# RWKV-7 chunks: level 5, the join, bonus and centring as 64x64 products on other quarters of the array

## What is computed

```python
def step(S, inp):                              # per token and head, S is 64 x 64
    sa = einsum('hvk,hk->hv', S, -kk_t)
    S = S * w_t[:, None, :] + sa[..., None] * b_t[:, None, :] + v_t[..., None] * k_t[:, None, :]
    o = einsum('hvk,hk->hv', S, r_t)
mu = mean(o, -1); var = mean(square(o - mu), -1)              # over the 64 of a head
o = (o - mu) * rsqrt(var + LNX_EPS) * lnx_w + lnx_b
bonus = sum(r_h * k_h * r_k, -1) * v_h                        # over the 64 of a head
y_a = (o + bonus) * g
```

## Time and profile before

| | |
|---|---|
| median of 3 runs | 2398.39 us (2395.95 to 2399.4) |
| the profiled execution | 2397.87 us |
| its span | 2396.1 us |
| mean granted TensorE clock | 0.994 |
| PE, DVE, ACT, POOL busy in the span | 98%, 57%, 30%, 51% |

### The profile page before, as it was taken

One profiled execution on the slowest core, in us unless ns is written; L12 is line 12 of the kernel. 1 busy time (PEld: TensorE's weight loads), 2 busy tenths in 40 slices (PEclk: granted clock), 3 DMA queues, 4 the chain that ended last, 5 costly groups with the idle time before them and its releaser, 6 DMA issues. The chain is left out here.

```text
span 2396.1 us, 51987 instructions
## 1 busy us (share of the span) xinstructions
PE 2353.7 (98%) x21980; PEld 2299.4 (96%) x21980; DVE 1366.3 (57%) x1939; ACT 715.0 (30%) x1358; POOL 1230.1 (51%) x846
## 2 busy tenths in 40 slices
PE   8999999999999999999999999999999999999998
PEld 8999999999999999999988888899999999999997
DVE  6666666588754455652566665576744444552235
ACT  6433333311020000112446766223433333330001
POOL 3868787644443345223322212254778777765640
PEclk9999999999999999999999999999999999999999
DMA  5212222433333523833451010262222222153212
GB/s 212 92 62 82 85 88 88 177 126 126 106 119 138 107 89 125 152 91 122 152 178 34 19 34 4 96 235 80 80 80 79 79 79 79 61 199 102 78 47 71
DMA packets 121703, 242.83 MB, mean 101 GB/s; under 512 B 35640, under 2 KB 61880, under 8 KB 120896
## 3 DMA queue, kind: packets, MB, share of 16 engines
q1 hardware_dynamic: 94128, 189.67, 24.1%
q10 hardware_dynamic: 27408, 50.76, 6.9%
HBM read 173.94 MB, written 65.29 MB: 100 GB/s over the span
## 5 line engine op out<-in xcount | busy, mean ns | idle before, releaser
L172 POOL TENSOR_TENSOR whi<-wraw,small 128x1024 fp32r<-128x1024 f32 (+1 forms) x60 | 105.2, 1753 | 407.7 <-PE ps L206 316.2
L206 PE MATMUL ps<-hhi,whi 128*128 128x344 f32 x816 | 177.2, 326 | 0.0
L206 PE MATMUL ps<-hlo,whi 128*128 128x344 f32 x816 | 173.6, 321 | 0.0
L206 PE MATMUL ps<-hhi,wlo 128*128 128x344 f32 x816 | 173.0, 320 | 0.0
L4053 PE MATMUL ps<-t_hi,whi 128*128 128x258 f32 x704 | 143.7, 285 | 3.0 <-ACT ffn_gate L3960 1.0
L175 POOL TENSOR_TENSOR wlo<-wraw,whi 128x1024 fp32r<-128x1024 f32 (+1 forms) x60 | 144.1, 2402 | 4.7
L4053 PE MATMUL ps<-t_lo,whi 128*128 128x258 f32 x704 | 142.1, 283 | 0.0
L4053 PE MATMUL ps<-t_hi,wlo 128*128 128x258 f32 x704 | 141.3, 282 | 0.0
L933 PE MATMUL ps<-t_hi,whi 128*128 128x258 f32 x672 | 136.4, 284 | 2.7 <-ACT ffn_gate L829 1.3
L206 PEld LDWEIGHTS ps<-hhi,whi 128*128 128x128 f32 x816 | 136.4, 189 | 2.1 <-issue 0.7
L206 PEld LDWEIGHTS ps<-hlo,whi 128*128 128x128 f32 x816 | 138.4, 190 | 0.0
(11 more groups left out here) (607 smaller groups left out, 6692.2 us busy)
## 6 DMA issues: line engine op xcount, KB each, us to landing
weights_raw_b<-ffn_up SPq DMA_DIRECT2D x22, 1024.0 KB, 5.0
wraw<-ffn_up SPq DMA_DIRECT2D x21, 1024.0 KB, 4.9
a_spilled<-ffn_gate SPq DMA_DIRECT2D x39, 516.0 KB, 2.7
a_raw<-a_spilled SPq DMA_DIRECT2D x39, 516.0 KB, 4.1
wraw<-ffn_down SPq DMA_DIRECT2D x48, 384.0 KB, 3.2
wraw<-w_mix SPq DMA_DIRECT2D x18, 512.0 KB, 3.5
gates<-gate_out ACTq DMA_DIRECT2D x16, 516.0 KB, 3.5
wraw<-w_gates SPq DMA_DIRECT2D x16, 512.0 KB, 3.9
```

What stands on the lines that cost most here:

```text
L172: pool.tensor_tensor(g.whi[:, s, 0:n], g.wraw[:, s, 0:n], g.zero.to_broadcast([P, n]), ALU.add).then_inc(g.w_hi, 1)
L206: last = pe.matmul(g.ps[:, 3 * bank_set + b, 0:BLK], w[:, s, k * P:(k + 1) * P], x(k, b), start=(k == 0 and first), stop=(k == kt - 1 and ...
```

## The change

Level t is written in another place of the two banks (`levels`), in the order `SWAP` of heads, with the T of head p stored at place `turned(p)`. From level 4 on, heads 2 and 3 have the second block on the other half (their second product of t4 goes across, too), so that level 5 and the join find heads 0 and 1 on two quarters and heads 2 and 3 on the two others. Level 5's t step is a function of its own, `level_end`. The join's first product (`join`) goes to bank 2, two heads of a group to lo and two to hi; its second (`joined`) is issued in the next turn, on PE behind lora and before the scores, on ACT first of all, for both groups together. The products with block diagonal matrices are issued as two 64x64 products, one for each half.

```diff
-JOIN = ["x60", "x61", "t60", "t61"]
+JOIN = ["x6", "t6"]
+SWAP = (0, 2, 1, 3)
...
+    def turned(p):
+        return (p + 2) % 4
+
+    def levels(n, j):
+        at = (tb(n) * 8 + (2 if j == 4 else 4)) * N
+        return g.ps[:, :, :].rearrange("p b c -> p (b c)")[:, at:at + 8 * N]
+
+    def ends(n, first, size):
+        return g.ps[:, tb(n):tb(n) + 2, first * N:(first + size) * N]
+
+    def inverse(n, p):
+        at = (3 * (p // 2) + p % 2) * N
+        return g.T2[lo, n].rearrange("p x a c -> p (x a c)")[:, at:at + N]
+
+    def low_end(n, p):
+        at = (5 if p < 2 else 2) * N
+        return g.T2[lo, n].rearrange("p x a c -> p (x a c)")[:, at:at + N]
...
@@ ACT, level @@
-                    act.activation(flat(g.T2[lo, n, 0]), g.ps[lo, tb(n), 0:4 * N], ACT.Copy)
-                    for r in (lo, hi):
-                        ins = act.activation(g.TTF[r, c % 2, 4 * n:4 * n + 4, r], half(tb(n) + 1, 0)[r], ACT.Copy)
+                    ins = act.activation(g.T2[lo, n].rearrange("p x a c -> p (x a c)")[:, 0:6 * N]
+                                         .rearrange("p (b c) -> p b c", b=2), ends(n, 0, 3)[lo], ACT.Copy)
@@ ACT, join @@
             for n in range(2):
-                inv["pe"].wait(act, c, f"x6{n}")
-                q_ev.on(act.activation(flat(g.XJ[hi, n]), g.ps[hi, tb(n), 0:4 * N], ACT.Copy), f"x6{n}")
-            for n in range(2):
-                inv["pe"].wait(act, c, f"t6{n}")
-                q_ev.on(act.activation(g.TTF[lo, c % 2, 4 * n:4 * n + 4, hi], half(tb(n), 1)[lo], ACT.Copy), f"t6{n}")
+                for r in (hi, lo):
+                    act.activation(g.TTF[r, c % 2, 4 * n:4 * n + 4, r].rearrange("p (b a) c -> p b a c", b=2),
+                                   ends(n, 3, 2)[r].rearrange("p b (a c) -> p b a c", a=2), ACT.Copy)
+            inv["pe"].wait(act, c, "x6")
+            q_ev.on(act.activation(g.XJ[:, :, :, :].rearrange("p n a c -> p (n a c)"), g.ps[:, 2, 0:4 * N], ACT.Copy),
+                    "x6")
+
+        def joined(c):
+
+            inv["pe"].wait(act, c, "t6")
+            q_ev.on(act.activation(g.TTF[lo, c % 2, :, hi].rearrange("p (m b) c -> p b m c", b=2),
+                                   g.ps[lo, 6:8, 0:4 * N].rearrange("p b (m c) -> p b m c", m=4), ACT.Copy), "t6")
@@ ACT, turn @@
+            if s is not None:
+                joined(s)
             if p is not None:
                 decay(p)
@@ DVE, level: at level 5 the masked copy reads ends(n, 0, 2), two blocks from each of two banks @@
@@ PE, bonus (centre, sample_sa and sample_centre in the same way) @@
-                last = pe.matmul(g.ps[:, prep_bank(d), p * CH:p * CH + w], g.blkrk[:, p, :], RK[:, p, 0:w],
-                                 start=True, stop=True)
+                for q in range(2):
+                    last = pe.matmul(g.ps[rows(q), prep_bank(d), p * CH:p * CH + w], g.blkrk[rows(q), p, rows(q)],
+                                     RK[rows(q), p, 0:w], start=True, stop=True)
@@ PE, scores: p < 2 @@
-                inv["act"].wait(pe, c - 1, "t61")
+                inv["act"].wait(pe, c - 1, "t6" if p else "x6")
@@ PE, level_x @@
-                for p in range(4):
+                for p in SWAP:
                     for r, other in ((lo, hi), (hi, lo)):
-                        last = pe.matmul(g.ps[other, tb(n), p * N:(p + 1) * N], g.SC[r, c % 2, 4 * n + p, 1, 0, r],
-                                         T[r, n, 0, p, :], start=True, stop=True)
+                        stays = j == 5 and p >= 2
+                        at = (p - 2 if stays else p) * N
+                        last = pe.matmul(g.ps[r if stays else other, tb(n) + stays, at:at + N],
+                                         g.SC[r, c % 2, 4 * n + p, 1, 0, r], T[r, n, 0, p, :], start=True, stop=True)
@@ PE, level_t, now for j < 5 @@
+                to = levels(n, j)
+                for p in SWAP:
+                    k = p if j == 1 else turned(p)
                     for r, other in ((lo, hi), (hi, lo)):
+                        pe.matmul(to[r, p * N:(p + 1) * N], T[other, n, 1, k, :], g.X[other, j - 1, n, p, :],
+                                  start=True, stop=True)
+                    at = (4 + turned(p)) * N
                     for r, other in ((lo, hi), (hi, lo)):
+                        last = pe.matmul(to[r if j == 4 and p >= 2 else other, at:at + N], g.X[other, j - 1, n, p, :],
+                                         T[other, n, 1, k, :], start=True, stop=True)
@@ PE, new @@
+        def level_end(c):
+
+            for n in range(2):
+                inv["dve"].wait(pe, c, f"x5{n}")
+
+                def pair_of(p, r):
+                    home = (r if p >= 2 else (hi if r == lo else lo))
+                    return g.X[home, 4, n, p, :], g.T2[home, n, 1, turned(p), :]
+
+                def to(r, b, k):
+                    return g.ps[r, tb(n) + b, k * N:(k + 1) * N]
+
+                for p in SWAP:
+                    X, T = pair_of(p, lo)
+                    pe.matmul(to(lo, p // 2, p % 2), T, X, start=True, stop=True)
+                for p in SWAP:
+                    X, T = pair_of(p, hi)
+                    pe.matmul(to(hi, p // 2, 3 + p % 2), X, T, start=True, stop=True)
+                for p in SWAP:
+                    X, T = pair_of(p, lo)
+                    last = pe.matmul(to(lo, p // 2, 3 + p % 2), X, T, start=True, stop=True)
+                for p in (1, 3):
+                    X, T = pair_of(p, hi)
+                    last = pe.matmul(to(lo, 1 - p // 2, 2), X, T, start=True, stop=True)
+                q_ev.on(last, f"t5{n}")
@@ PE, join and joined @@
+            if c:
+                state["dve"].wait(pe, c - 1, "s")
+            if c == NCH - 1:
+                sam["dve"].wait(pe, 0, "u3")
             for n in range(2):
                 inv["act"].wait(pe, c, f"t5{n}")
+                for p in PAIRS:
+                    at = (2 * n + p // 2) * N
+                    last = pe.matmul(g.ps[lo if p % 2 else hi, 2, at:at + N], g.SC[lo, c % 2, 4 * n + p, 1, 0, hi],
+                                     inverse(n, p), start=True, stop=True)
+            q_ev.on(last, "x6")
+
+        def joined(c):
+
+            inv["act"].wait(pe, c, "x6")
             for n in range(2):
+                for p in PAIRS:
+                    at = (2 * n + p // 2) * N
+                    if p % 2:
+                        last = pe.matmul(g.ps[lo, 7, at:at + N], g.XJ[lo, n, p // 2, :], low_end(n, p),
+                                         start=True, stop=True)
+                    else:
+                        last = pe.matmul(g.ps[lo, 6, at:at + N], g.XJ[hi, n, p // 2, :],
+                                         g.TTF[hi, c % 2, 4 * n + p, hi], start=True, stop=True)
+            q_ev.on(last, "t6")
```

More of the change, by code:

```diff
@@ L2082, in plan_rwkv @@
     assert o - 4 * 2 * 4 * CH <= g.s5_off + 4 * 2 * J * CH, (o, g.s5_off + 4 * 2 * J * CH)
-    g.XJ, o = g.at("rw_xj", o, [P, 2, 4, N])
+    g.XJ, o = g.at("rw_xj", o, [P, 2, 2, N])
     g.T2, o = g.at("rw_t", o, [P, 2, 2, 4, N])
@@ L2380, in level @@
                 if j < 5:
-                    ins = act.activation(g.T2[:, n].rearrange("p x a c -> p x (a c)"),
-                                         g.ps[:, tb(n):tb(n) + 2, 0:4 * N], ACT.Copy)
-                else:
-                    act.activation(flat(g.T2[lo, n, 0]), g.ps[lo, tb(n), 0:4 * N], ACT.Copy)
-                    for r in (lo, hi):
-                        ins = act.activation(g.TTF[r, c % 2, 4 * n:4 * n + 4, r], half(tb(n) + 1, 0)[r], ACT.Copy)
+                    ins = act.activation(g.T2[:, n].rearrange("p x a c -> p (x a c)"), levels(n, j), ACT.Copy)
+                else:
+                    ins = act.activation(g.T2[lo, n].rearrange("p x a c -> p (x a c)")[:, 0:6 * N]
+                                         .rearrange("p (b c) -> p b c", b=2), ends(n, 0, 3)[lo], ACT.Copy)
                 q_ev.on(ins, f"t{j}{n}")
@@ L2637, in level @@
                 inv["pe"].wait(v, c, f"x{j}{n}")
-                st.do(v.copy_predicated(g.X[:, j - 1, n], mask(j), half(tb(n), 0)))
+                if j < 5:
+                    st.do(v.copy_predicated(g.X[:, j - 1, n], mask(j), half(tb(n), 0)))
+                else:
+                    st.do(v.copy_predicated(g.X[:, j - 1, n].rearrange("p (b a) c -> p b a c", b=2),
+                                            mask(j).rearrange("p (b a) c -> p b a c", b=2),
+                                            ends(n, 0, 2).rearrange("p b (a c) -> p b a c", a=2)))
                 q_ev.mark(v, f"x{j}{n}")
@@ L2908, in level_t @@
                 inv["dve"].wait(pe, c, f"x{j}{n}")
-                for p in range(4):
+                to = levels(n, j)
+                for p in SWAP:
+                    k = p if j == 1 else turned(p)
                     for r, other in ((lo, hi), (hi, lo)):
-                        if j < 5 or r == lo:
```

(31 more changed lines are left out.)

## The result

The change makes the kernel slower. Before, timed again beside it, took 2396.7 us (median of 5, 2395.88 to 2399.4), after 2407.27 us (median of 5, 2406.61 to 2411.13): a ratio of 1.0044, 95% interval 1.0033 to 1.0056, 10.6 us more. The forecast was 2396.3 us with a range up to 2402.5, so it was wrong, and the sign with it. The profiled execution took 2411.13 us, its span 2409.3 us, at a mean granted clock of 0.990 where it was 0.994.

What follows compares the result with a forecast made beforehand. Despite PE's 98% busy, ACT before level 4 and DVE's run to "bv" were taken to limit steady turns. Seven turn ends at +0.10 (+0.7) and the last turn's -2.8 gave -2.1: 2396.3 us, range 2388.5 to 2402.5.

Steps and rivals of the forecast that it cites:

- the sign: Whole kernel: -2.1 us, slightly faster; chances 0.21 faster, 0.63 within 0.2%, 0.16 slower.
- PE and ACT arrive together at level 4, so the centring is worth 0: Between levels 2 and 4: ACT's copy, exponentials, copy fix the time, so 0.67 us less PE work gains 0.
- Level 4 and level 5's x step cancel: Level 4's t step makes the sums 0.22 later; level 5's shorter x step keeps the masked copies' end unchanged.
- The rule of the Trainium skill: Level 5's x step: different row tiles cannot share a PSUM bank; if so, 1.6 us more, 2397.9; forecast rejected it.
- A wait at lora for DVE in place of PE's work, of 2.0 to 2.5 us, released by "bv": Turn end: about 2.3 us of wait replaces about 2.9 us of PE work; gain at lora 0.70.
- The moved join, 0.80: Join's second product between lora and scores: 0.47 of records plus 0.33 of bubbles, +0.80 us a turn.
- +0.10 us a turn: Steady turn's sum: -0.70 at lora and +0.80 for the moved join; seven turn ends give +0.7.
- The last turn, -2.8: Last turn, PE is the path: 3.2 us saved, 0.4 taken off for the join's waits; bounds -1 to -4.
- the wait itself was costed at nothing: New 2.3 us PE wait before lora: the forecast's own case gave it no clock cost; that case had 0.64.
- the fall of the clock: Rival: the new 2.3 us stand lowers the clock; two falls decide for slower, seven give about 2428; chance 0.08.
- The row taken as the precedent: Profile row at full clock (1.00) across 7 us with PE idle 2.3, cited against the clock falling at lora.
- The price of one fall: Clock rival: a fall to half level lasts 9 us and costs 4.5 us.

Runs made afterwards that it cites:

- e3: Kernel after, with DVE's bonus product ("bv") moved ahead of the inverse decayed keys: 2386.91 us, ratio to before 0.9961.
- e1: Kernel after, plus eight extra 128x128x128 products on PE in the wait ahead of lora: 2397.08 us, ratio to before 0.9996.
- e10: Kernel after, plus four extra 128x128x128 products on PE in the wait ahead of lora: 2399.97 us in its only execution.
- e2: Kernel before, with only bonus, centring and the two sample products issued as 64x64 pairs: 2395.45 us, ratio to before 0.999.
- e9: Kernel before, with only DVE's bonus product ("bv") moved ahead of the inverse decayed keys: 2396.98 us, ratio to before 0.9998.
- e14: Kernel before, with only the bonus issued as 64x64 pairs: 2397.25 us, ratio to before 1.000.
- e6: Kernel after, with bonus, centring and sample products as 128x128 products again, levels and join kept: 2406.29 us, ratio to before 1.0035.

## Why the prediction was wrong

- **PE and ACT arrive together at level 4, so the centring is worth 0.** Right: 0.54 us of wait where about 0.6 was expected, and 35.08 us a turn with the centring alone.
- **Level 4 and level 5's x step cancel.** Right. From level 4's start to the sums it was 2.83 and is 3.06 us, +0.23 where 0.22 was expected; from level 4's start to the masked copies it was 4.13 and is 4.16. The 32 records of level 5's x step are through in 0.69 us where one such step took 1.15, though both row halves of the array write each of the two banks; 0.69 is what eight records on each of four quarters take at 0.058. The rule of the Trainium skill (TensorEngine Tiling (Array Packing), Gotcha 1: PSUM Pressure), by which they could not, does not hold here for different partitions of a bank.
- **A wait at lora for DVE in place of PE's work, of 2.0 to 2.5 us, released by "bv".** Right: 2.2 to 2.5 us in the seven turns.
- **The moved join, 0.80.** Near: lora to scores is 1.70 us at full clock (e3, 1293.47 to 1295.17) against 0.99, +0.71; at half clock it is 2.15.
- **+0.10 us a turn.** A clean turn has +0.16. DVE's run from the copies' end to "bv" is 4.32 us instead of 4.20, which the sum did not have.
- **The last turn, -2.8.** Right as work: with the wait filled (e1) it is 37.11 instead of 39.09, that is -1.98 with the join's 0.7 to 0.8 ahead of the scores, so about -2.7 behind them. Its parts were not measured one by one. In the kernel after, the fall at its start takes it back.
- **The step that failed: the wait itself was costed at nothing**, "as long, in one piece, with dense work on both sides", and the fall of the clock stood among the rivals with 0.08. Both reasons for so low a chance were wrong. The row taken as the precedent, seven microseconds with 2.3 of them idle at 1.00, does not carry over: its idle time lies in two pieces, of which the longer is 1.81 us, and one piece of 2.2 to 2.5 has a fall behind it here in 5 of 7 turns. Timeline of PE, kernel before, in that stretch:

```profile
1233.59 1.16 PE L2808 MATMUL ps<-rw_lora,rw_wa 64*128 64x128 f32 x16 [1.81 <-issue]
```

  And dense work behind the wait is no protection; it is what the fall slows. Lora, the join and the scores are on the path, PE is never idle in them, and all of the half clock is paid.
- **The price of one fall was mis-sized too**, from the only falls at hand in the earlier trace rows, of 9 us and more: 4.5 us each. It is 3.4 us of half clock, 1.7 us lost. So two falls would not have decided for slower; four of 3.4 and one of 6.8 did. They make the sum: turns -1 and 0 cancel (-0.78, +0.82); turns 1 to 5 have four falls of 1.7, 0.8 of the stall named below, and five times the clean turn's 0.16, together 8.4 (measured 8.5 for all seven). The last turn has -1.98 and a fall of 6.8, +3.4, that is +1.4 (measured +1.0).

What the experiments show is that the loss is the falls (e1 takes them away in the steady turns and keeps every step of the change) and that in this kernel they come with the wait at lora (e1 and e10 fill it, e3 shortens it). What stays open is the exact condition. The Trainium skill (TensorE: Matmul & The Clock Gate, Part 1) says that the gate follows how busy PE has been lately; the falls behind the waits agree with it. But two of the seven waits, of 2.2 and 2.5 us, had none behind them, one of the falls of e2 came behind 2.63 busy microseconds of 3.2, and that of e9 behind 3.35 of 3.40. Whether the array's unused quarters count, which e2, e14 and e9 suggest, was not tried by itself: no run fills the wait with 64x64 products on one quarter.

## What to carry to other kernels

A wait of TensorE is not free even where nothing is late for it, since its granted clock can fall: here 10 of the 13 waits of 2 us or more at lora (after, e6) had a half clock behind them, in work on the path, nine of 3.4 us at about 1.7 us each and one of 6.8, and a single stretch without a fall was weak evidence against it. When a change takes work off PE ahead of a wait, look first at what the wait is for; here another order of two parts on DVE turned the same change from +0.44% into -0.4%. And before a saving is counted, ask for each step which engine arrives second, by how much: centring 0 of 0.67, bonus 0.43 of 0.66, the levels 0 as long as DVE came last.

## What the runs showed of the hardware

- Inside the turns the half clock lasts 3.4 us, once 6.8 in the kernel after. It began from 0.1 us ahead of lora's start (e6, 1370.03) to 2.3 us behind it (e10, 1479.67), so it lies almost wholly in work and not in the wait.
- A product can start before one that is issued ahead of it for another quarter. In the kernel after, the two other heads' bonus pairs (L2878) are issued behind the level-5 t step and begin while its last products still run. Timeline of PE, kernel after:

```profile
1334.22 0.23 PE L2978 MATMUL ps<-rw_t,rw_x 64*64 64x64 f32 x2
1334.23 0.32 PE L2878 MATMUL ps<-rw_e,rw_blkrk 64*64 64x128 f32 x1
1334.28 0.22 PE L2978 MATMUL ps<-rw_t,rw_x 64*64 64x64 f32 x2
```

- In 8 of the 13 traces one turn, not always the same, has an extra 0.8 to 1.1 us of "issue" ahead of `o`, with no releaser in the trace; turn 3 of the kernel after has it (38.10 us). Its cause was not looked for.
